# Two feature chunks, the compressed probabilities' transposes and a taken-apart gelu inside attention's first blocks

## What is computed

```python
def mixer(h, ...):
    u = h @ w_in
    (x_lru, y_lru, q_dn, kv_dn, k_pe, q_n, kc, vc, ks, vs, kw, vw, g_n) = split(u)
    a_out = recurrent_group(x_lru, y_lru, ...)   # rg_lru(conv(x_lru)) * gelu(y_lru)
    b_out = mla_group(...)                       # 6 heads, causal attention
    c_out = nsa_group(...)                       # 6 heads: compressed, selected, window branch
    return concatenate([a_out, b_out, c_out], -1) @ w_out

def nsa_group(...):
    ...
    p_c = masked_softmax(s_c, cmp_end[None, :] <= qpos[:, None])   # 31 compressed keys
    o_c = einsum('bgpqn,bngd->bqgpd', p_c, vc)
    ...
    return gate0 * o_c + gate1 * o_s + gate2 * o_w
```

## Time and profile before

| | us |
|---|---|
| median of 3 runs | 1524.36 (1523.14 to 1525.96) |
| the profiled execution, its own time | 1521.68 |
| its span, first to last instruction | 1519.9 |
| PE busy | 1383.6 (91%) |
| DVE busy | 943.1 (62%) |
| ACT busy | 701.0 (46%) |
| POOL busy | 87.9 (6%) |
| mean granted PE clock | 0.963 of full |

### The profile page before, as it was taken

How to read it: one execution, slowest core, us unless ns; L and a number is a source line. 1 busy time by engine, 2 the same in 40 slices (tenths; PEclk the granted TensorE clock), 3 DMA queues, 4 the chain that set the end, 5 groups by cost and what they waited for, 6 DMA issues and landing times.

```text
span 1519.9 us, 27360 instructions
## 1 busy us (share of the span) xinstructions
PE 1383.6 (91%) x11638; PEld 910.0 (60%) x11638; DVE 943.1 (62%) x1416; ACT 701.0 (46%) x1079; POOL 87.9 (6%) x85
## 2 busy tenths in 40 slices
PE   4999799989999999988998998879999999999992
PEld 1346455434444444433355554369999999999982
DVE  5774777465430354127854775477677788888885
ACT  3434676234310332014245663165555566666662
POOL 0010200320000000120000000400000000000002
PEclk9999899999999999998999799979999999999997
DMA  5430581315320432006220000147678788899985
GB/s 186 177 98 28 187 295 60 124 62 189 125 83 1 157 137 107 0 0 223 77 70 27 2 1 12 45 173 285 223 265 290 281 314 323 310 340 339 346 296 181
DMA packets 37143, 244.65 MB, mean 161 GB/s; under 512 B 5224, under 2 KB 6632, under 8 KB 22560
## 3 DMA queue, kind: packets, MB, share of 16 engines
q1 hardware_dynamic: 30064, 216.74, 39.0%
q0 software_dynamic: 6816, 25.69, 5.2%
q10 hardware_dynamic: 144, 0.52, 0.1%
HBM read 214.40 MB, written 26.44 MB: 158 GB/s over the span
## 4 chain that ended last, share of the span: by engine, by line
PE 74%; DVE 12%; ACT 7%; issue 4%; DMA 2%; SPq 0%; POOL 0%; POOLq 0%; DVEq 0%; ACTq 0%
PE bank L959 17%; PE bank L961 17%; PE bank L960 17%; PE bank L1138 4%; ACT arena L671 3%; PE bank L1164 2%; PE bank L1192 2%; DVE arena L791 2%; PE bank L564 2%; PE bank L563 2%; PE bank L565 2%; PE bank L529 2%; DVE arena L1517 1%; ACT arena L1444 1%; DVE small L1783 1%
## 5 line engine op out<-in xcount | busy, mean ns | idle before, releaser
L791 DVE SCALAR_TENSOR_TENSOR arena<-arena 128x3072 f16<-128x3072 f32 x86 | 288.8, 3358 | 77.6 <-ACT arena L671 77.5
L671 ACT ACTIVATE arena<-arena 128x3072 f16<-128x3072 f32 x86 | 237.0, 2756 | 0.7 <-DMA arena<-in_ew 0.6
L959 PE MATMUL bank<-arena 128*128 128x512 bf16 (+4 forms) x880 | 211.2, 263 | 7.6 <-DVE arena L1581 4.4
L961 PE MATMUL bank<-arena 128*128 128x512 bf16 (+4 forms) x880 | 211.2, 263 | 0.0
L960 PE MATMUL bank<-arena 128*128 128x512 f16 (+4 forms) x880 | 211.1, 263 | 0.0
L959 PE MATMUL bank<-hh,wring_hi 128*128 128x512 bf16 x352 | 135.3, 384 | 23.1 <-DVE hl L1531 18.4
L563 PE MATMUL bank<-arena 128*128 128x128 bf16 (+5 forms) x704 | 139.9, 229 | 1.1 <-DVE arena L824 1.1
L959 PE MATMUL bank<-hh,arena 128*128 128x512 bf16 x352 | 134.0, 381 | 6.5 <-DVE hl L1531 6.5
L565 PE MATMUL bank<-arena 128*128 128x128 bf16 (+5 forms) x704 | 139.9, 229 | 0.0
L564 PE MATMUL bank<-arena 128*128 128x128 f16 (+5 forms) x704 | 139.9, 229 | 0.0
L959 PE MATMUL bank<-wring_hi,arena 128*128 128x128 bf16 (+2 forms) x704 | 133.8, 226 | 5.5 <-DVE arena L791 4.7
(11 more groups left out here) (283 smaller groups left out, 2557.0 us busy)
## 6 DMA issues: line engine op xcount, KB each, us to landing
arena<-in_ew SPq DMA_DIRECT2D x86, 1536.0 KB, 8.4
arena<-in_dw SPq DMA_DIRECT2D x22, 1536.0 KB, 6.5
wstage<-in_w_chunk SPq DMA_DIRECT2D x44, 512.0 KB, 3.6
expert_results<-iota POOLq DMA_DIRECT2D x9, 2048.0 KB, 20.9
arena<-in_cmp_w SPq DMA_DIRECT2D x2, 2048.0 KB, 9.7
expert_results<-wstage SPq DMA_DIRECT2D x7, 512.0 KB
arena<-in_w_tok SPq DMA_DIRECT2D x2, 1096.0 KB, 5.9
xT<-in_x SPq DMA_DIRECT2D x4, 512.0 KB, 5.3
```

The source lines that it names most:

```text
L671: act.activation(ew_hi_[:, G % EP, :], ew[:, G % ES, :], ACT.Copy, scale=SW).then_inc(M["hi_ready"], 1)
L791: dve.scalar_tensor_tensor(out=ew_lo_[:, G % EP, :], in0=ew[:, G % ES, :], scalar=SW, in1=ew_hi_[:, G % EP, :], op0=ALU.mult, op1=ALU.subt ...
L959: pe.matmul(out, w_hi, x_hi, start=first, stop=False)
L961: return pe.matmul(out, w_lo, x_hi, start=False, stop=last)
```

## The change

Chunks 12 and 13 and `turn_cmp` leave `PREPARE` and are done between the first steps of attention, into the two banks of attention's outputs (`out_bank`), which are free until the first `values`. `LATE_STEP` puts chunk 12 behind `scores(1)` and chunk 13 behind `scores(2)`, `turn_cmp` behind `turn(0)` in step 3. The gelu is taken apart: POOL makes `y + 0.044715*y**3` in three operations for each of two chunks, ACT does `Tanh` in step 10, DVE the rest in `lru_finish`, which moves from step 4 to step 12 and has one more operation for each chunk.

```diff
-    ("feat", 12), ("turn_cmp", 0),
-    ("feat", 13), ("gelu_y", 0),
 ]
+LATE = [j for j, f in enumerate(FEAT) if f[0] == "y"]
+LATE_STEP = {1: LATE[0], 2: LATE[1]}
+TURN_CMP_STEP, TANH_STEP, FINISH_STEP = 3, 10, 12
...
+                def late_feat(j):
+                    J = NW * l + j
+                    pe.wait_ge(*ready("w_lo", J))
+                    for k in range(KC):
+                        mm = product(out_bank[j % 2][:, :], ...)
+                    mm.then_inc(*signal("w_used", J))
...
-                        b = take(("pct", l, h), ("pct", l, h))
+                        b = out_bank[h % 2]
+                        pe.wait_ge(*(ready("feat", l, LATE[h]) if h < 2 else ready("pct", l, h - 2)))
...
+                    if g in LATE_STEP:
+                        late_feat(LATE_STEP[g])
                     if g >= 3:
                         turn(g - 3)
+                        if g == TURN_CMP_STEP:
+                            turn_cmp()
...
-                        act.wait_ge(*ready("feat", l, feat_index("y", c)))
-                        ins = act.activation(yl[:, c, :], yl[:, c, :], ACT.Gelu_apprx_tanh)
+                        act.wait_ge(*ready("gelu_in", l, c, 2))
+                        ins = act.activation(tmp[:, 2 + c, :], tmp[:, 2 + c, :], ACT.Tanh, scale=GELU_ROOT)
...
                     if g < ND:
                         exps(g)
+                    if g in LATE_STEP:
+                        feat(LATE_STEP[g])
+                    if g - 1 in LATE_STEP:
+                        w_hi(NW * l + LATE_STEP[g - 1] + WR)
                     if g >= 3:
                         turned(g - 3)
+                    if g == TURN_CMP_STEP:
+                        turn_cmp()
+                    if g == TANH_STEP:
+                        gelu_y()
...
-                        link(dve.tensor_tensor(tmp[:, c, :], tmp[:, c, :], yl[:, c, :], ALU.mult))
+                        link(dve.scalar_tensor_tensor(out=yl[:, c, :], in0=tmp[:, 2 + c, :], scalar=1.0, in1=yl[:, c, :],
+                                                      op0=ALU.add, op1=ALU.mult))
+                        link(dve.scalar_tensor_tensor(out=tmp[:, c, :], in0=tmp[:, c, :], scalar=0.5, in1=yl[:, c, :],
+                                                      op0=ALU.mult, op1=ALU.mult))
...
+                    if g - 2 in LATE_STEP:
+                        feat(LATE_STEP[g - 2])
-                    if g == TT:
+                    if g == FINISH_STEP:
                         lru_finish()
...
                         pool.dma_start(blank[:, a:a + n, :], iota[:, 0:256].unsqueeze(1).broadcast_to([P, n, 256])
                                        ).then_inc(*signal("blank", by=16))
+                for c in range(LC):
+                    y, u = yl[:, c, :], tmp[:, 2 + c, :]
+                    pool.wait_ge(*ready("feat", l, feat_index("y", c)))
+                    pool.wait_ge(*ready("lru_scanned", l, c))
+                    pool.tensor_tensor(u, y, y, ALU.mult).then_inc(*signal("gelu_in", l, c, 0))
+                    pool.wait_ge(*ready("gelu_in", l, c, 0))
+                    pool.tensor_scalar(u, u, 0.044715, 1.0, ALU.mult, ALU.add).then_inc(*signal("gelu_in", l, c, 1))
+                    pool.wait_ge(*ready("gelu_in", l, c, 1))
+                    pool.tensor_tensor(u, u, y, ALU.mult).then_inc(*signal("gelu_in", l, c, 2))
                 pool.wait_ge(*ready("lru_out", l, LC - 1))
```

More of the change, by code:

```diff
@@ L65 @@
 NEG = -1.0e30
+GELU_ROOT = 0.7978845608028654
 SCALE_MLA = float(DQK) ** -0.5
@@ L1002, in feat @@
                     mm.then_inc(*signal("w_used", J))
+                def late_feat(j):
+                    J = NW * l + j
+                    pe.wait_ge(*ready("w_lo", J))
+                    for k in range(KC):
+                        mm = product(out_bank[j % 2][:, :], wring_hi[:, J % WR, k, :], wring_lo[:, J % WR, k, :],
+                                     hh[:, k, :], hl[:, k, :], k == 0, k == KC - 1)
+                    mm.then_inc(*signal("w_used", J))
                 def tok(i):
@@ L1097, in lru_gates, with turn_cmp @@
                                   stop=True).then_inc(*signal("lru_mm", l, c, w))
-                def turn_cmp(_):
+                def turn_cmp():
                     pe.wait_ge(*ready("pc", l))
                     for h in range(HEADS):
-                        b = take(("pct", l, h), ("pct", l, h))
+                        b = out_bank[h % 2]
+                        pe.wait_ge(*(ready("feat", l, LATE[h]) if h < 2 else ready("pct", l, h - 2)))
                         for i in range(TT):
@@ L1109, in _ @@
                         "uk": uk, "uv": uv, "hid": compress_hidden, "cmp": compress_out, "cmp_scores": cmp_scores,
-                        "lru_gates": lru_gates, "turn_cmp": turn_cmp}
+                        "lru_gates": lru_gates}
                 for step, which in PREPARE:
@@ L1313, in feat @@
                     act.wait_ge(*ready("w_used", NW * l + j))
-                    b = bank[ring_of[("feat", l, j)]]
+                    b = out_bank[j % 2] if j in LATE else bank[ring_of[("feat", l, j)]]
                     if (name, c) == ("qdn", 1):
@@ L1321, in feat @@
                                    ).then_inc(*signal("feat", l, j))
-                    w_hi(NW * l + j + WR)
+                    if j not in LATE:
+                        w_hi(NW * l + j + WR)
                 def wtok_upper(_):
@@ L1377, in compress_out, with gelu_y @@
                         act.copy(vcs[0:NCMP, :], b[0:NCMP, 0:2 * HD]).then_inc(*signal("cmp", l, s))
-                def gelu_y(_):
+                def gelu_y():
                     for c in range(LC):
-                        act.wait_ge(*ready("feat", l, feat_index("y", c)))
-                        ins = act.activation(yl[:, c, :], yl[:, c, :], ACT.Gelu_apprx_tanh)
+                        act.wait_ge(*ready("gelu_in", l, c, 2))
+                        ins = act.activation(tmp[:, 2 + c, :], tmp[:, 2 + c, :], ACT.Tanh, scale=GELU_ROOT)
                     ins.then_inc(*signal("gelu_y", l))
@@ L1419, in lru_root, with turn_cmp @@
                                        ACT.Sqrt).then_inc(*signal("lru_root", l, c))
-                def turn_cmp(_):
+                def turn_cmp():
                     for h in range(HEADS):
                         act.wait_ge(*ready("pct_mm", l, h))
-                        act.copy(PTc[0:NCMP, h, :],
-                                 bank[ring_of[("pct", l, h)]][0:NCMP, :]).then_inc(*signal("pct", l, h))
+                        act.copy(PTc[0:NCMP, h, :], out_bank[h % 2][0:NCMP, :]).then_inc(*signal("pct", l, h))
                 part = {"feat": feat, "tok": tok, "wtok": wtok_upper, "squares": latent_squares, "norm": latent_root,
-                        "uq": uq, "uk": uk, "uv": uv, "hid": compress_hidden, "cmp": compress_out, "gelu_y": gelu_y,
+                        "uq": uq, "uk": uk, "uv": uv, "hid": compress_hidden, "cmp": compress_out,
                         "gates": gates_sigmoid, "lru_gates": lru_gates, "lru_decay": lru_decay, "cmp_max": cmp_max,
-                        "lru_root": lru_root, "turn_cmp": turn_cmp}
+                        "lru_root": lru_root}
                 for step, which in PREPARE:
@@ L1761, in lru_scan @@
                         link(dve.tensor_tensor(ix, ix, tmp[:, 2 + c, :], ALU.mult))
-                        link(dve.tensor_tensor_scan(tmp[:, c, :], xl[:, c, 0:T], ix, 0.0, ALU.mult, ALU.add))
+                        scanned = dve.tensor_tensor_scan(tmp[:, c, :], xl[:, c, 0:T], ix, 0.0, ALU.mult, ALU.add)
+                        scanned.then_inc(*signal("lru_scanned", l, c))
                 def lru_finish():
```

1 line of the change is left out of this document (added).

## The result

The kernel after takes **1551.78 us** as a median of 4 runs (1548.92 to 1559.06), the kernel before 1523.75 us (1522.67 to 1525.96) beside it. The ratio is 1.0195, with a 95% interval of 1.0174 to 1.0216: 28 us slower. The forecast was 1551, in a range of 1541 to 1565.

A forecast was written before the change was run, and what follows sets the result against it. PE, busy for 91% of the span, was taken as the bound. The profiled 1521.7 us plus 25 (layer 0) and 2 (layer 1) gave 1548.7, as a median 1551 us, in a range of 1541 to 1565.

The forecast's parts named there:

- seven issues, then three ending at: POOL, layer 0: seven zero-writing DMA issues go out, POOL waits, the last three end at 215.2 us.
- exponentials 11: ACT, layer 0: standing behind the tanhs that wait for POOL, they come at 222.7 us instead of 198.81.
- chunk 13 through: PE, attention's opening in layer 0: chunk 13, largely at full clock, ends near 170.7 us.
- exponentials 8: ACT, layer 0: they come near 188.7 us, 2.8 us earlier, or less if idle keeps PE's clock down.
- layer 0: Whole layer 0: +25 us, from +24 for POOL's hold and +1 for what follows it.
- layer 1: Whole layer 1, without zero writes: +2 us, bounds -3 and +9, with `lru_finish` at 3 us.
- The hold: POOL, layer 0: it stands 41.19 us at the eighth zero-writing issue, which starts 6.5 us earlier with the first maximum.
- Rival (A): POOL, layer 0: not really held, gelu inputs ready by 181 us; 1516 us, or 1528 if the clock falls; chance 0.10.
- Rival (B): POOL, layer 0: arithmetic begins only when all zero writes have landed, 13 us more, 1564 us; chance 0.10.
- Rival (C): POOL, layer 0: the hold is 5 to 15 us shorter, 1536 to 1546 us; chance 0.08 for below 1541.
- Rival (D): Attention's opening: not earlier, first issue stays at 169, 1557 us; no own chance, included in the forecast's 0.72.
- 2 us gained at step 8: Attention, both layers: exponentials 8 come 2 us earlier, bounds 0 and 4, after an opening 8.7 us earlier.

The follow-up runs named there:

- experiment 1: Kernel after the change, with POOL's gelu arithmetic put ahead of the ten zero-writing DMA issues in layer 0: 1536.51 us, ratio 1.0079.
- experiment 2: Kernel after the change, with layer 0's gelu arithmetic on POOL put between the seventh and eighth zero-writing issues: 1528.79 us, one run.
- experiment 3: Kernel after the change, with layer 0's gelu arithmetic on POOL put between the eighth and ninth zero-writing issues: 1556.33 us, one run.
- experiment 9: experiment 6 with the zero writes cut into 19 issues of 1 MB at most instead of ten of 2 MB at most: 1511.24 us, one run.
- experiment 5: experiment 4 with DVE's two scans done in step 1, behind the first maxima instead of ahead of them: 1515.07 us, ratio 0.9959.
- experiment 6: experiment 5 with the late chunks' upper weight halves on ACT moved to steps 5 and 6, DVE's remainders to 6 and 7: 1512.02 us, ratio 0.9925.
- experiment 4: experiment 1 with `lru_finish` divided by chunk onto steps 28 and 32 instead of one piece in step 12: 1526.86 us, ratio 1.0024.
- experiment 7: Kernel before with only gelu taken apart: POOL's products ahead of its zero writes, tanhs in step 10, `lru_finish` in steps 28 and 32: 1515.71 us, ratio 0.9949.

## Why the prediction was right, and where it was not

| step | predicted | measured |
|---|---|---|
| seven issues, then three ending at | 215.2 | 217.42 |
| six gelu operations, last ends | 6.7 us, 222 | 6.2 us, 223.7 |
| exponentials 11 | 222.7 | 224.24 |
| first exponentials, layer 0 | 162.6 | 162.99 |
| chunk 13 through | 170.7 | about 172.6 |
| scores 4 | 178.0 | 180.76 |
| exponentials 8 | 188.7 | 192.47 |
| layer 0 | +25 | +25.2 |
| layer 1 | +2 | +10.2 (experiments 1 to 3: +4.9, +1.9, +8.8) |
| median | 1551 | 1551.78 |

**The hold was read rightly, and decides.** That POOL is held at the eighth issue, that the hold moves with the first maximum, and that ACT, in order, takes everything behind it along: all three came as worked out. Experiments 2 and 3 show the cause, experiment 1 what it costs (15.3 us between the medians, where what it uncovers is left in). Rival (A) falls: with the arithmetic behind all the issues, POOL was not free before 196. By the rule of the Trainium skill (DMA: Bandwidth & Descriptors, Issuing engines are not separate DMA queues), an issue costs only the sequencer's time, usually small beside the transfer. Of the seven issues before the hold and the fifteen of experiment 9 this is true (1.15 and 0.91 us each), of the next one it is not. Rival (B) falls: the arithmetic followed the last issue by 0.1 us. Rival (C) falls: the hold was 43.03 us, not shorter. Rival (D) falls: the opening came 8.3 us earlier. One price of the sum was read across two kinds of product: the 1649 ns of the earlier trace rows are those of L1976, which cost 1.26 us at 649.44 and 2.13 at 951.61 before, not those of L1969. The six operations came out at 6.2 us all the same, for the scalar forms took 0.61 and 0.62.

**The step that failed: 2 us gained at step 8.** None came, in either layer: exponentials 8 were 1.0 us later in layer 0 (192.47 against 191.45, of which ACT was 0.7 us late at 149 already) and 0.6 us later in layer 1. By the forecast's own marks this was to show the step wrong, and so was a layer 1 that is off by over 5 us. The wait (4.12 us, predicted 4.7) and the fall of the clock were expected. Mis-sized was how long the clock stays down: I took it back after 1.5 to 3.5 us of dense matmuls, from the kernel's opening, and it stayed at 0.50 from 163.5 to 169. That made chunk 13 2 us later. The kernel before shows, in the same place, longer ones still, two stretches with PE busy for most of them:

```profile
171.00:183.00 12.00, 10.16 (x46) 6.78 (x48) 8.70 (x24) 6.42 (x25) 6.36 (x6) 0.50 0.99 331
836.00:852.00 16.00, 13.92 (x62) 9.23 (x64) 12.14 (x36) 9.63 (x36) 0.00 (x0) 0.50 0.01 2
```

Then it fell a second time, behind the 2.72 us in the turned probabilities: the last eight transposes took 1.71 us instead of 1.10, and scores 4 took 0.80 us instead of 0.49. From scores 4 to exponentials 8 it took 11.7 us; I had put 10.7 from 178.0, 1 us short. The forecast's own text had this case ("if the 2.6 us of idle keep the clock down") at 1 to 2 us less than 2.8; it was 3.1 less in layer 0 (without the 0.7) and 3.4 in layer 1. Experiments 5 and 6 show the price as a whole: with the two pauses shortened and less of the half clock, the kernel is 14.8 us faster than experiment 4.

**The term that was mis-sized: layer 1.** `lru_finish` was priced at 3 us for its time on DVE. It is 5.1 us in one piece, PE pauses 3.30 us, and then comes the half clock, which stood in no term. Experiment 4 shows it: 9.6 us less for both layers with the same work in two pieces and later, and the clock at 1.00 there.

How long the half clock lasts behind this pause of 3.30 us differs between executions of the same lists. It was over 13 us in after's layer 1, in experiment 1's layer 0 and in experiment 3's layer 1; it was 3 to 4 us in experiment 1's layer 1 and in both layers of experiment 2. Layer 1's mixer took 328.5 and 327.1 us with the long one, 323.2 and 320.2 with the short one, against 318.4 before. So the forecast's +2 is what experiment 2's execution shows (+1.9), and after's shows +10.2. What decides between the two lengths, no run here shows.

This is also why the median came out within 1 us of the forecast: that is in part luck. Taken on its own execution, the forecast's 1548.7 stands against 1559.06, 10 us short, and 8 of them are layer 1's. The two fastest runs of after (1548.92 and 1549.34) have a mean clock of 0.958 against this one's 0.952. That fits a half clock of the short kind in them, but they have no trace, and it stays a reading.

**What the change would have been worth.** Repaired, the change pays: experiment 6 beats both kernels. How much of that the late chunks bring is not clear of the noise: experiment 7, without them, is at 1515.71 us, 3.7 us behind experiment 6, and the 95% intervals of the two ratios overlap. Four places in queues cost the change 40 us: the arithmetic behind the zero writes (15.3), `lru_finish` in one piece in step 12 (9.6), the scans ahead of the first maxima (11.8), the weights' halves ahead of the evictions (3.0); each is the difference of two medians, taken in this order, and the last is smaller than the spread of the runs.

## What to carry to other kernels

When work is given to an engine that also issues transfers, look for where that engine stands with no releaser named, and put the work ahead of it: here the queue was full after seven transfers, and the next issue held everything behind it. When a stage's opening is brought forward, read what else stands ahead of it on each engine, since the old opening may have hidden it (here two scans). And a pause of 3 to 4 us of the matrix engine is priced with the half clock behind it, read from the same place of the kernel and from more than one execution: the same pause was followed here by 3 us of it or by 13.

## What the runs showed of the hardware that was not expected

- GpSimd's transfer queue took 14 MB in seven transfers, or 15 MB in fifteen, with rows of 1 KB; the next one held GpSimd for 41 to 43 us in every kernel (36.25 us of plain idle in experiment 2, where the arithmetic filled the first part). Room doesn't come free with each transfer that lands: the hold ends about when all are drained, and then the rest go out at once. In after the DMA share was 0.20 in 212 to 214 and 0.00 in 214 to 216, and the eighth issue came at 214.36; the nine 2 MB transfers took 21.7 us from issue to landing in the median, so some of the seven had landed long before.
- PE's clock stayed at 0.50 over more than 5 us of busy matmuls behind a wait of 4.12 us, and over 12 us behind one of 3.30 us, in after. In experiments 1 and 2 the same wait of 3.30 us was also followed by only 3 to 4 us of it. A pause of 1.78 us left the clock at full in layer 0 of experiment 6 and was followed by over 3 us at 0.50 in its layer 1.
- A scalar form with two steps costs GpSimd 0.61 to 0.62 us for 128x512 where a product costs 1.04 to 1.27 us with DVE little at work; in experiment 6, beside DVE's scan, the first product took 1.33 us and the first scalar form 1.40.
- DVE's scan of 128x512 took 1.95 us instead of 1.23 with GpSimd at work beside it (experiment 5, the second scan; the first took 1.23).
